# Joined changes to the attention stage of a hybrid encoder block: meta query pieces in slots 1, 2 and 4, an LRU output tile five placed ahead of the last meta product, head 0 prepared in another order, and head 1's queries split by VectorE

## The reference, cut to what matters

```python
h = concat([meta (16 tokens), x (1024 tokens)])          # (1, 1040, 1024)
proj = rmsnorm(h, norm_mix_g) @ w_in
x_lru, g_lru, c_q, c_kv, k_pe = split(proj)
y_lru = rg_lru_bidir(dwconv(x_lru)) * gelu(g_lru)
q = rope(rmsnorm((rmsnorm(c_q) @ w_uq) per head, q_norm_g))      # 8 heads x 96
k, v = from rmsnorm(c_kv) @ w_ukv and rope(k_pe)                 # k normalised per head
y_mla = softmax(q @ k.T / sqrt(96)) @ v                          # all 1040 keys, per head
y = concat([rmsnorm(y_lru), rmsnorm(y_mla)])
h = h + y @ w_out
gate, up = split(rmsnorm(h, norm_ffn_g) @ w_ffn_up)
h = h + (silu(dwconv(gate)) * up) @ w_ffn_down
return h[:, 16:]
```

## Time and profile before

| | us |
|---|---|
| runs shown | 1299.99, 1302.21 (median), 7115.12 |
| the profiled execution: its own time | 1303.02 |
| its span | 1301.2 |
| TensorE busy | 1271.2 |
| VectorE busy | 996.9 |
| ScalarE busy | 769.3 |
| GpSimd busy | 146.6 |

### The profile page before, as it was taken

How to read it: one execution, slowest core, us unless ns; L and a number is a source line. 1 busy time by engine, 2 the same in 40 slices (tenths; PEclk the granted TensorE clock), 3 DMA queues, 4 the chain that set the end, 5 groups by cost and what they waited for, 6 DMA issues and landing times.

```text
span 1301.2 us, 18506 instructions
## 1 busy us (share of the span) xinstructions
PE 1271.2 (98%) x6158; PEld 1018.6 (78%) x6158; DVE 996.9 (77%) x1505; ACT 769.3 (59%) x1156; POOL 146.6 (11%) x175
## 2 busy tenths in 40 slices
PE   7999999899999999999999999999999999999998
PEld 7999997666666666687678888888888888888886
DVE  6677569678887876577779887887878887887855
ACT  7487648567765866534445565656474565656460
POOL 3000037400000001322200000000010000000010
PEclk9999999999999999999999999999999999999999
DMA  6111200000000014200144846576574847576667
GB/s 220 34 53 41 74 1 1 1 1 10 9 9 10 9 58 155 69 30 1 49 148 94 187 100 166 118 169 134 151 169 93 189 97 169 113 170 133 157 143 245
DMA packets 40938, 123.01 MB, mean 95 GB/s; under 512 B 7378, under 2 KB 8082, under 8 KB 34484
## 3 DMA queue, kind: packets, MB, share of 16 engines
q0 software_dynamic: 7200, 52.43, 21.4%
q1 hardware_dynamic: 33684, 69.86, 15.7%
HBM read 62.34 MB, written 59.80 MB: 94 GB/s over the span
## 4 chain that ended last, share of the span: by engine, by line
PE 85%; DVE 6%; ACT 5%; issue 2%; DMA 1%; POOL 0%; SPq 0%; DVEq 0%; ACTq 0%
PE banks L2911 30%; PE banks L2983 14%; PE banks L100 7%; PE banks L102 7%; PE banks L101 7%; PE banks L1935 2%; PE banks L2040 2%; PE banks L2041 2%; PE banks L2042 2%; PE banks L2060 2%; PE banks L2063 2%; PE banks L2061 2%; ACT e_f L1558 1%; PE banks L1895 1%; ACT e_h L1565 1%
## 5 line engine op out<-in xcount | busy, mean ns | idle before, releaser
L2911 PE MATMUL banks<-x_hi,slot_h 128*128 128x512 f32 x616 | 242.8, 394 | 2.5 <-DVE slot_l L2599 1.3
L2911 PE MATMUL banks<-x_lo,slot_h 128*128 128x512 f32 x616 | 243.4, 395 | 0.0
L2911 PE MATMUL banks<-x_hi,slot_l 128*128 128x512 f32 x616 | 242.9, 394 | 0.0
L2384 ACT ACTIVATE slot_h<-up_raw 128x512 fp32r<-128x512 f32 x127 | 79.8, 629 | 174.4 <-PE banks L2911 172.3
L2911 PEld LDWEIGHTS banks<-x_hi,slot_h 128*128 128x128 f32 x616 | 115.6, 188 | 30.9 <-DVE slot_l L2599 2.1
L2911 PEld LDWEIGHTS banks<-x_lo,slot_h 128*128 128x128 f32 x616 | 115.7, 188 | 27.1
L2911 PEld LDWEIGHTS banks<-x_hi,slot_l 128*128 128x128 f32 x616 | 115.7, 188 | 26.9
L2462 ACT ACTIVATE staged<-banks 128x1024 f32<-128x1024 f32 x100 | 101.4, 1026 | 41.0 <-PE banks L2983 41.0
L2983 PE MATMUL banks<-dn_h,a_h 128*128 128x512 f32 x280 | 110.4, 394 | 0.0
L2983 PE MATMUL banks<-dn_h,a_l 128*128 128x512 f32 x280 | 109.5, 391 | 0.0
L2983 PE MATMUL banks<-dn_l,a_h 128*128 128x512 f32 x280 | 109.5, 391 | 0.0
(11 more groups left out here) (346 smaller groups left out, 2861.5 us busy)
## 6 DMA issues: line engine op xcount, KB each, us to landing
down_sums<-staged POOLq DMA_DIRECT2D x50, 1024.0 KB, 8.0
up_raw<-in_w_up SPq DMA_DIRECT2D x88, 256.0 KB, 3.3
dn_raw<-in_w_down SPq DMA_DIRECT2D x22, 512.0 KB, 6.6
win_raw<-in_w_in SPq DMA_DIRECT2D x11, 512.0 KB, 3.3
x_tm<-in_x_tm SPq DMA_DIRECT2D x8, 512.0 KB, 6.0
wo_raw<-in_w_out SPq DMA_DIRECT2D x16, 256.0 KB, 4.1
h<-in_x_tm SPq DMA_DIRECT2D x8, 512.0 KB, 5.7
down_sums<-h SPq DMA_DIRECT2D x3, 1024.0 KB, 6.6
```

The lines of the kernel that those rows point to most:

```text
L2384: nc.scalar.activation(s_h[slot], x, ACT.Copy).then_inc(sem["up_hi"], 1)
L2911: ins = nc.tensor.matmul(o, s[slot][:, k], xs[w], start=fresh and k == 0 and n == 0, stop=k == 3 and n == 2, skip_group_check=not fresh)
```

## The change

It is a join of five edits, all in `attention_out_phase`:

- "x0", "x1", "x2" of head h move from slots 1, 1, 2 of head h to slots 1, 2, 4. For head 0, where they stood before the first scores, they go to slots 2, 4, 5 of head 0. For head 7 they go from slots 4, 5, 6 of head 6 to 5, 6, 8. On the SP queue `last_queries(h)` goes behind `recip_row(h-1)`, and in head 6 behind the four reads of `w_out` too; for head 7 it still stands ahead of the row.
- `lru_products(4)` is placed in step (8, 1), ahead of the last meta product; the splits of tiles 6 and 7 and the additions of tiles 4 to 6 are put earlier or later around it.
- Head 0 is prepared in the order tq0, tk0, tq1, tk1, a0 to a7, tm, a8 to a15, am, r, over all eight banks, with waits of its own for each job (`HEAD_0`), two identity products a score job, and others ahead of jobs. The first two slots' scores are made before the row is there (`scores_ahead`): 12 products of 96 rows, then 4 products of the one row.
- In slots 0 and 1 of head 0, TensorE has no scores; `keep_busy(2)` stands there four times. Head 1's queries are transposed at slot 0, places 2 and 3.
- Their high parts are made by VectorE (`SPLIT_BY_DVE`).

```diff
--- before.py
+++ after.py
@@ -1077,10 +1077,13 @@
     LAST_AHEAD = dict(PREPARE)
-    LAST_AHEAD.update({4: ("a5", "x0", "a6", "a7"), 5: ("a8", "x1", "a9", "a10"), 6: ("a11", "x2", "a12", "a13")})
-    FIRST = dict(PREPARE)
-    FIRST.update({8: ("x0", "x1", "x2", "")})
-    OWN = {1: ("", "", "x0", "x1"), 2: ("", "x2", "", "")}
+    LAST_AHEAD.update({5: ("a8", "x0", "a9", "a10"), 6: ("a11", "x1", "a12", "a13"), 8: ("x2", "", "", "")})
+    FIRST = {0: ("tq0", "tk0", "tq1", "tk1"), 1: ("a0", "a1", "a2", "a3"), 2: ("a4", "a5", "a6", "a7"),
+             3: ("tm", "a8", "a9", "a10"), 4: ("a11", "a12", "a13", "a14"), 5: ("a15", "am", "r", "")}
+    OWN = {1: ("", "", "x0", ""), 2: ("", "x1", "", ""), 4: ("", "x2", "", "")}
+    SECOND = dict(PREPARE)
+    SECOND.update({0: ("", "", "tq0", "tq1"), 1: ("", "", "", "tk0")})
+    OWN_FIRST = {2: ("", "x0", "", ""), 4: ("", "x1", "", ""), 5: ("", "x2", "", "")}
@@ -1089,9 +1092,10 @@
         places = [None] * 4
-        ahead = FIRST if h < 0 else LAST_AHEAD if h == END - 1 else PREPARE
-        for plan, head in [(ahead, h + 1), (META_QUERIES, h), (LRU_SUMS, h), (OWN, h)]:
-            if plan is OWN and not 1 <= h < END:
+        ahead = FIRST if h < 0 else SECOND if h == 0 else LAST_AHEAD if h == END - 1 else PREPARE
+        own = OWN if h else OWN_FIRST
+        for plan, head in [(ahead, h + 1), (META_QUERIES, h), (LRU_SUMS, h), (own, h)]:
+            if plan is own and not 0 <= h < END:
@@ -1104,8 +1108,10 @@
     first = len([j for s in range(SLOTS) for j in side_jobs(-1, s) if j])
+    side_banks = [2, 3, 6, 7, 0, 1, 4, 5] + [(6, 7, 4, 5, 2, 3, 0, 1)[n % 8] for n in range(first - 9)] + [4] +\
+                 [6 + n % 2 for n in range(len(jobs) - first)]
     BY_ACT = {"r", "x0", "x1", "x2"}
-    LOWS = [("tq0", 0), ("tq1", 0), ("tk0", 0), ("tk1", 0)]
+    LOWS = [("tq0", 0), ("tk0", 0), ("tq1", 0), ("tk1", 0)]
@@ -1117,23 +1123,19 @@
+        return bank(side_banks[number[j]], 1)
+    def before(j):
         n = number[j]
-        if n >= first - 3 and n < first:
-            return bank(4 + (n - first + 3) % 2, 1)
-        return bank([6, 7, 2, 3, 0, 1][n % 6] if n < first else 6 + (n - first) % 2, 1)
-    def before(j):
-        n = number[j]
-        if n < first - 3:
-            return jobs[n - 6:n - 5] if n >= 6 else []
-        if n < first:
-            return jobs[n - 2:n - 1] if n == first - 1 else []
-        return jobs[n - 2:n - 1] if n > first + 1 else [("r", 0), ("am", 0)]
+        return [i for i in jobs[:n] if side_banks[number[i]] == side_banks[n]][-1:]
+    SPLIT_BY_DVE = [("tq0", 1), ("tq1", 1)]
+    FIRST_KEYS = [("a0", 0), ("a1", 0), ("a2", 0), ("a3", 0)]
...
-        return sum(HIGH.get(i[0], 0) for i in jobs[:number[j]])
+        return 2 if j in FIRST_KEYS else sum(HIGH.get(i[0], 0) for i in jobs[:number[j]] if i not in SPLIT_BY_DVE)
@@ -1267,7 +1269,8 @@
     side_x, side_y = side_of(("xt", END)), side_of(("xo", END))
-    L_SLOT = {3: 0, 4: 1, 6: 2, 7: 3}
+    L_SLOT = {(END, 3): 0, (END, 4): 1, (END, 6): 2, (END, 7): 3}
+    L_GAP = 4
@@ -1317,10 +1320,6 @@
-            if h == END:
-                sp.wait_ge(sem["ysum"], 4)
-                for k in range(4):
-                    sp.dma_start(raw_of(k), dram["w_out"][P * k:P * k + P, 0:half]).then_inc(sem["wo_a"][k], 16)
@@ -1330,14 +1329,18 @@
               .then_inc(sem["row_in"], 16)
-            if h != END:
-                last_queries()
...
                 recip_row(sp, h - 1)
+            if h == END - 1:
+                sp.wait_ge(sem["ysum"], 4)
+                for k in range(4):
+                    sp.dma_start(raw_of(k), dram["w_out"][P * k:P * k + P, 0:half]).then_inc(sem["wo_a"][k], 16)
+            if h != END:
+                last_queries()
@@ -1423,6 +1426,8 @@
             side = side_of(j)
+            if j in SPLIT_BY_DVE:
+                return
@@ -1538,6 +1543,7 @@
             if h == HEADS and s == 2:
+                split_y("L", 6)
@@ -1571,8 +1577,8 @@
             split_w(m)
-        split_y("L", 6)
-        split_y("L", 7)
+            if m == LF + 1:
+                split_y("L", 7)
@@ -1674,15 +1680,17 @@
             if (h, s) == (HEADS, 1):
+                add_lru(L_GAP)
...
                 split_w(5)
-                add_lru(4)
...
             side = side_of(j)
-            if kind in HIGH:
+            if j in SPLIT_BY_DVE:
+                dve.wait_ge(sem["side_done"], number[j] + 1)
+            elif kind in HIGH:
@@ -1694,6 +1702,8 @@
                     dve.wait_ge(sem["rope_done"], NT)
+                if j in SPLIT_BY_DVE:
+                    link(nc.vector.tensor_scalar(hi[0:QK, cs], side[0:QK], gain[kind[1]], None, ALU.mult))
@@ -1770,13 +1780,14 @@
                 if h == HEADS:
+                    add_lru(5)
...
                     split_w(7)
-                    add_lru(5)
-                    add_lru(6)
...
                 nc.vector.tensor_tensor(y_of(h - 1), rb, o_sb[0:VD], ALU.mult).then_inc(sem["y_mul"], 1)
+                if h == HEADS:
+                    add_lru(6)
@@ -1896,8 +1907,10 @@
     def tensor(pe):
-        WARM = {"tk0": 10, "am": 8}
-        WARM.update({f"a{n}": 1 for n in range(2 * XT)})
+        WARM = {"tq0": 2, "tk0": 2, "tq1": 4, "tk1": 2, "a0": 6, "r": 2}
+        WARM.update({f"a{n}": 2 for n in range(2, 2 * XT)})
+        HEAD_0 = {"tq0": (8, 4, 4, 0), "tk0": (8, 4, 4, 0), "a0": (NT, 0, 0, 0), "a1": (NT, 0, 0, 0),
+                  "tq1": (8, 8, 8, 0), "tk1": (8, 8, 8, 0)}
@@ -1908,12 +1921,13 @@
                 wait_read(pe, i)
-            if number[j] < 6 or j == ("tm", 0):
-                done = {"tq0": 8, "tq1": 8, "tk0": 8, "tk1": 8}.get(kind, NT)
-                pe.wait_ge(sem["q_scaled"], done)
-                pe.wait_ge(sem["kv_read"], done)
-                pe.wait_ge(sem["rope_done"], done)
-                pe.wait_ge(sem["v_full"], done)
+            if number[j] < 8 or j == ("tm", 0):
+                for name, done in zip(("q_scaled", "kv_read", "rope_done", "v_full"), HEAD_0.get(kind, (NT,) * 4)):
+                    if done:
+                        pe.wait_ge(sem[name], done)
+            if h == 0 and kind in WARM:
+                for _ in range(WARM[kind]):
+                    nc.tensor.matmul(side[:, 0:P], ident, ident, start=True, stop=True)
@@ -1930,6 +1944,8 @@
+                if j == ("a0", 1):
+                    wait_read(pe, ("tq1", 1))
@@ -1963,11 +1979,6 @@
             ins.then_inc(sem["side_done"], 1)
-            if h == 0 and kind in WARM:
-                if kind == "a0":
-                    pe.wait_ge(sem["kv_read"], NT)
-                for _ in range(WARM[kind]):
-                    nc.tensor.matmul(bank(3 if kind == "tk0" else 5)[:, 0:P], ident, ident, start=True, stop=True)
@@ -2023,8 +2034,8 @@
                 meta_pv(s, i)
-            if h == END and s in L_SLOT:
-                lru_products(L_SLOT[s], i)
+            if (h, s) in L_SLOT:
+                lru_products(L_SLOT[h, s], i)
@@ -2042,6 +2053,30 @@
                 ins.then_inc(sem["s_done"], 1)
+        def scores_ahead():
+            pe.wait_ge(sem["b_set"], 2 + len(LOWS))
+            for g in range(2):
+                ks = slice(P * g, P * g + P)
+                for c in range(2):
+                    cs = slice(512 * c, 512 * c + 512)
+                    out = s_ps(g)[:, cs]
+                    nc.tensor.matmul(out, k_h[0][0:QK, ks], q_h[0][0:QK, cs], start=True, stop=False)
+                    nc.tensor.matmul(out, k_h[0][0:QK, ks], q_l[0][:, cs], start=False, stop=False)
+                    nc.tensor.matmul(out, k_l[0][:, ks], q_h[0][0:QK, cs], start=False, stop=False)
+            pe.wait_ge(sem["row_in"], 16)
+            for g in range(2):
+                for c in range(2):
+                    cs = slice(512 * c, 512 * c + 512)
+                    ins = nc.tensor.matmul(s_ps(g)[:, cs], k_h[0][QK:QK + 1, P * g:P * g + P], q_h[0][QK:QK + 1, cs],
+                                           start=False, stop=True)
+                ins.then_inc(sem["s_done"], 1)
+        def keep_busy(n):
+            for _ in range(n):
+                nc.tensor.matmul(bank(5)[:, 0:P], ident, ident, start=True, stop=True)
@@ -2066,19 +2101,24 @@
             if (h, s) == (0, 0):
-                pe.wait_ge(sem["b_set"], 2)
+                scores_ahead()
...
             for c in range(2):
-                if 0 <= g < G:
+                if 2 <= g < G:
...
                 place_job(h, s, js, c)
+            if g - 2 == G - 1:
+                for k in range(LF):
+                    lru_products(L_GAP, k)
...
                     pv(g - 2, c)
+                elif 0 <= g < 2:
+                    keep_busy(2)
...
-        for j in range(4, XT):
+        for j in range(L_GAP + 1, XT):
```

## The result

The changed kernel takes 1303.78 us (median of 20 runs, 1302.05 to 1307.42), the kernel before 1300.62 in as many: a ratio of 1.0029, interval 1.0023 to 1.0036. (One run of the kernel before took 7115.12 us; the ratio is that of the others.) The forecast was 1300.4, 1.8 less than before: the time lies in its range of 1293 to 1306, the sign was wrong.

A forecast was written before the change was run, and what follows sets the result against it. TensorE, busy 1271.2 of 1301.2 us, was taken as the bound. Terms -2.7 - 4.2 + 5.6 + 1.5 + 1.4 - 3.4 = -1.8 took the median 1302.2 to 1300.4, range 1293 to 1306.

The forecast's parts named there:

- Meta pieces in heads 1 to 6: Slots 1, 2, 4: moving the pieces removes TensorE waits, 0.7 a head, -4.2 us in six heads, bounds -1.5 to -6.
- then finds the low part of tk1 just made: Heads 1 to 6: a0 no longer waits for tk1's low part, a wait put at 0.2 us before.
- Head 0: Head 0's new preparation order: first exponential 4.2 us earlier, slot 3 3.5 earlier, net -2.7, bounds -4.5 to 0.
- rival 3: Head 0 gains nothing, through added identity products or a clock fall: +2.7 on the sum, 1303.1, no change; chance 0.13.
- The queue in head 6: Slot 5: x0 copy waits behind last_queries and w_out reads; TensorE idles 5.6 us, then lower clock costs 1.5.
- the floor of 4.3: Head 6, slot 5: TensorE's shortest wait, 4.3 us, if the query copy lands at 478.4.
- Head 7's row: Start of head 7: row copy issued later, behind x2's copy and last_queries; TensorE waits +1.4 us, 0 to 2.5.
- The tail: Last meta product to group M 0: wait of 2.73 and low clock go; M 0 3.4 us earlier, bounds -4.3 to -2.
- The frame: Whole kernel: sums made against one profiled execution of 1303.0 us, taken as 0.8 above the median of 1302.2.
- Rival 2: Head 6's queue hurts more: wait 7.5, clock falls twice (3.0), row costs 2.9; +3.1, 1305.3; chance 0.17.

The follow-up runs named there:

- e10: Changed kernel with VectorE's sum over y of heads 2 to 4 in slot 3 in place of slot 1: 1302.76 us, ratio 1.0018.
- e13: e9 with VectorE's sum over y of heads 2 to 4 at the end of slot 8: 1294.36 us, ratio 0.9958.
- e5: Kernel before with only the tail's part of the change; head 0, meta pieces and SP queue as before: 1296.7 us, ratio 0.9973.
- e3: Changed kernel with head 7's product a9, just ahead of the 6.37 us wait, made 24 times in place of once: 1301.94 us, ratio 1.0019.
- e6: Changed kernel with ScalarE, not VectorE, making the high parts of head 1's queries: 1304.99 us in one run.
- e7: Changed kernel without the keep_busy identity products in slots 0 and 1 of head 0: 1306.13 us in one run.
- e1: Changed kernel with head 6's copy of the query pieces issued ahead of the four w_out reads: 1296.8 us, ratio 0.9978.
- e2: Changed kernel with two x_one buffers used in turn for the query pieces, SP queue order as changed: 1294.84 us, ratio 0.996.
- e4: Changed kernel with meta query pieces and SP queue from head 1 on as in the kernel before: 1297.05 us, ratio 0.9983.
- e11: Kernel before with twelve more identity products behind tk0 in head 0 (22 in place of 10): 1305.85 us in one run.
- e12: e9 with the sum over y of heads 2 to 4 in slot 8 and no keep_busy in head 0: 1296.66 us, ratio 0.9974.
- e9: Changed kernel, two x_one tiles, last_queries ahead of w_out reads in head 6, behind the row in head 7: 1295.41 us; again, 1295.76 us.
- e14: e9 without keep_busy in head 0: 1297.75 us, ratio 0.9985.

## Why the prediction was wrong, step by step

- **Meta pieces in heads 1 to 6, -4.2: the step that failed most.** The working for one head (1.05 lost before, 0.4 after) was right: head 1 gains 0.60, with a wait of 0.20 where I said 0.4. But a0 "then finds the low part of tk1 just made" holds in head 1 only. In heads 2 to 4 VectorE's sum over y, 1.22 us, stands ahead of that low part, and I hadn't looked at what VectorE does in slot 1 of each head: a gain of 0.15 each is left. Heads 1 to 5, for which I had -3.5, gave -1.08 + 0.49 = -0.6. The traces of e10 and e13 show the sum as the cause; the +0.49 of head 5 goes with the late row (0.55), a wait that no part of the forecast had.
- **Head 0, -2.7.** Measured -1.12 against a profiled execution that had 1.57 of low clock in this stretch, which I took for a part of the kernel; against e5 it is +0.45, just beyond the bound of 0 on this term. That is the outcome of rival 3, no gain from head 0, though not for its reason. In detail: "r" 242.5 (241.9 said), first exponential 246.3 (245.8), slot 3 at 255.3 (253.4). What I left out lies in slots 0 to 2: I costed VectorE's four operations on the queries at nothing, as it only waited there; they take 2.9 us, tk0's low part stands behind them and two more, and x0 waits 0.53 for it. That the row's products of one row cost as much as others (four in 1.2 us with their overlap) was the value taken.
- **The queue in head 6, +5.6 and +1.5.** Right in place, chain and sign: 6.37 in a10's bracket. The landing took 4.6 us from the issue (473.62 to 478.20), where I had 3.8. The clock was mis-sized: I took its 1.5 from seven slow products after a wait of 2.73; here it stayed low for 10 us, 6 of them with TensorE at work, 2.9 by e3. In the other three traces with this wait (5.8 to 6.3 us in e6, e7 and e10) it stayed low for 6.8, and row 6 to row 7 took 44.6 to 45.2 in place of 45.70, so the term itself differs from one execution to the next. On the Trainium skill's rule that a small copy need not complete behind a large one (DMA: Bandwidth & Descriptors, "Queues, rings and completion order"): here it came no sooner than 4.6 us after its issue behind the reads, and 2.9 ahead of them (e1, 471.86 to 474.75); the floor of 4.3 for the wait wasn't reached.
- **Head 7's row, +1.4.** TensorE waits 0.78. The whole of head 6 with its own 0.7 was to cost +7.8 and cost +9.36.
- **The tail, -3.4.** -3.9 from the last meta product to M 0, -4.4 from head 7's start. GpSimd's low part is the last wait, 0.26, as said.
- **The frame.** The rest, M 0 to the end, -1.0, is the end's two groups. The forecast's sum was made against one profiled execution whose own 1303.0 was 2.4 above the median of twenty: it held three stretches of low clock and a late end. -1.8 against it could have been near nothing against the median before any term was wrong.

Against the table: 2.9 too much in heads 1 to 5, 1.6 in head 0, 1.6 too little in head 6; the tail and the end give 2.0 back. That makes +2.3 of -1.8. Rival 2 named 3.1 us more, and 3.2 were measured, but that is luck: it wanted a wait of 7.5 in head 6, two falls of the clock and a row 2.9 late, with all the gains in place. The wait was 6.37, the clock fell once, the row cost 0.78, and the rest of the loss is gains that didn't come.

## What to carry to other kernels

Where a wait goes, look at what the engine that releases it does next to it in every repetition of the loop: heads 2 to 4 differed from head 1 by one operation of VectorE, and it took three quarters of the gain. The single small buffer here, freed by a copy on a shared queue, was cheap only while the queue's order kept big transfers behind that copy; a second buffer took 9 us off (e2 against the changed kernel). And before a term of one or two us is read from a profiled execution, find out whether that stretch is the same in another one.

## What the runs showed that I had not expected

- The clock falls in a busy stretch too, and not in every execution: at 420, 0.1 to 1.6 us behind the last of the 2-column products of "ys", it was low for some 3 us in the profiled executions of before, after, e1, e4, e7, e11 and e12, for about twice that in e2, e6 and e9 again, and not at all in e3, e5, e9, e10, e13 and e14. Head 5 is 35.8 to 39.7 long accordingly; of two with the wait for the row, e2's is 39.73 and e9's 36.96. e9 and e9 again are one kernel: the first had no such stretch, the second the long one.
- A wait of 1.19 us in head 0 (e14) and one of 2.66 in head 6 (e1) brought no fall in the profiled execution; one of 1.40 in head 0 did in that of before and not in that of e5.
- The kernel's last microseconds depend on one 1 MB load that lands 10 to 14 or 16 to 17 us after its issue.
